# Second layer's latent attention: no norm of the latents, heads in half tiles read from PSUM, query weights in buffers of their own

## What is computed

```python
cq, ckv, kr = jnp.split(h @ w_down, [Q_LORA, Q_LORA + KV_LORA], axis=-1)
q = (rms_norm(cq, qa_g) @ w_uq).reshape(B, S, H_B, QK_NOPE + QK_ROPE)
kv = (rms_norm(ckv, kva_g) @ w_ukv).reshape(B, S, H_B, QK_NOPE + V_DIM)
k_nope, v = kv[..., :QK_NOPE], kv[..., QK_NOPE:]
k = jnp.concatenate([k_nope, jnp.broadcast_to(kr[:, :, None, :], (B, S, H_B, QK_ROPE))], axis=-1)
q = rope_tail(rms_norm(q, q_g), QK_ROPE, cos[:, None, :], sin[:, None, :])
k = rope_tail(rms_norm(k, k_g), QK_ROPE, cos[:, None, :], sin[:, None, :])
```

## Time and profile before

| | us |
|---|---|
| median of three executions | 1251.47 |
| lowest and highest | 1250.41, 1252.01 |
| the profiled execution's own time | 1252.3 |
| its span in the trace | 1250.4 |
| PE busy in the span | 1215.3 |
| VectorE (DVE) busy | 763.2 |
| ScalarE (ACT) busy | 545.9 |
| POOL busy | 216.5 |

### The profile page before, as it was taken

The page is one execution under the profiler, slowest core; times in us unless marked ns, Lnnn a source line. Parts: engine busy times, 40 slices in busy tenths (PEclk is TensorE's granted clock), DMA queues, the critical chain, the costliest instruction groups (busy, mean ns, idle before and its releaser), DMA issues.

```text
span 1250.4 us, 17161 instructions
## 1 busy us (share of the span) xinstructions
PE 1215.3 (97%) x6052; PEld 971.6 (78%) x6052; DVE 763.2 (61%) x1315; ACT 545.9 (44%) x931; POOL 216.5 (17%) x262
## 2 busy tenths in 40 slices
PE   7999999999999999999999878999999999999998
PEld 5758876678788888878888766778788888887887
DVE  4588976646766565663337778763775656664334
ACT  5554345645534343333226676643543433343222
POOL 4423433411200000000004663430400000000000
PEclk9999999999999999999999999999999999999999
DMA  6522222212322222212233100012322222212323
GB/s 234 192 93 87 83 78 60 69 51 101 108 101 94 101 101 101 84 61 91 101 101 105 50 20 1 1 35 101 130 73 101 101 101 101 90 62 84 101 92 110
DMA packets 25120, 110.83 MB, mean 89 GB/s; under 512 B 2752, under 2 KB 3136, under 8 KB 17776
## 3 DMA queue, kind: packets, MB, share of 16 engines
q1 hardware_dynamic: 25072, 110.21, 25.5%
HBM read 108.06 MB, written 6.33 MB: 91 GB/s over the span
## 4 chain that ended last, share of the span: by engine, by line
PE 88%; DVE 6%; POOL 2%; issue 2%; ACT 2%; DMA 1%; SPq 0%; DVEq 0%; POOLq 0%; ACTq 0%
PE ps L1737 25%; PE ps L1739 24%; PE ps L1738 24%; PE ps L1498 3%; PE ps L1517 3%; PE ps L1388 2%; PE ps L1376 2%; DVE h_lo L954 1%; DVE xT L1151 1%; DVE w_lo L948 1%; PE ps L1371 1%; PE ps L1482 1%; PE ps L1410 1%; PE ps L1709 1%; POOL rope_tmp L490 1%
## 5 line engine op out<-in xcount | busy, mean ns | idle before, releaser
L948 DVE TENSOR_TENSOR w_lo<-raw,w_hi 128x1024 fp32r<-128x1024 f32 (+4 forms) x114 | 195.2, 1712 | 260.9 <-ACT w_hi L582 260.9
L1737 PE MATMUL ps<-h_hi,w_hi 128*128 128x512 f32 (+1 forms) x712 | 278.6, 391 | 2.5 <-DVE w_lo L948 2.5
L582 ACT ACTIVATE w_hi<-raw 128x1024 fp32r<-128x1024 f32 (+4 forms) x124 | 177.8, 1434 | 230.3 <-PE ps L1739 230.3
L1738 PE MATMUL ps<-h_lo,w_hi 128*128 128x512 f32 (+1 forms) x712 | 277.8, 390 | 0.0
L1739 PE MATMUL ps<-h_hi,w_lo 128*128 128x512 f32 (+1 forms) x712 | 277.8, 390 | 0.0
L1737 PE MATMUL ps<-a_hi,w_hi 128*128 128x512 f32 x480 | 188.0, 392 | 2.1 <-DVE w_lo L948 1.6
L1738 PE MATMUL ps<-a_lo,w_hi 128*128 128x512 f32 x480 | 186.8, 389 | 0.0
L1739 PE MATMUL ps<-a_hi,w_lo 128*128 128x512 f32 x480 | 186.8, 389 | 0.0
L1737 PEld LDWEIGHTS ps<-h_hi,w_hi 128*128 128x128 f32 (+1 forms) x712 | 133.6, 188 | 32.1 <-DVE w_lo L948 3.4
L1738 PEld LDWEIGHTS ps<-h_lo,w_hi 128*128 128x128 f32 (+1 forms) x712 | 133.7, 188 | 28.3 <-issue 0.6
L1739 PEld LDWEIGHTS ps<-h_hi,w_lo 128*128 128x128 f32 (+1 forms) x712 | 133.5, 188 | 28.4 <-issue 0.7
(11 more groups left out here) (188 smaller groups left out, 1510.7 us busy)
## 6 DMA issues: line engine op xcount, KB each, us to landing
raw<-in_f_up SPq DMA_DIRECT2D x44, 1024.0 KB, 4.8
raw<-in_f_w_down SPq DMA_DIRECT2D x44, 512.0 KB, 3.3
raw<-in_a_in_wide SPq DMA_DIRECT2D x13, 1024.0 KB, 4.8
bias_tiles<-bias_rows SPq DMA_DIRECT2D x1, 4096.0 KB, 19.7
raw<-in_a_w_out SPq DMA_DIRECT2D x8, 512.0 KB, 3.2
raw<-in_b_w_out SPq DMA_DIRECT2D x8, 512.0 KB, 3.3
xT<-in_xt SPq DMA_DIRECT2D x4, 512.0 KB, 6.5
toep_b<-bias_tiles SPq DMA_DIRECT2D x8, 256.0 KB, 3.2
```

Of the source, the lines that this page charges most:

```text
L582: sc.activation(w_hi[:, s, 0:n], raw[:, s, 0:n], ACT.Copy).then_inc(w_hi_done, 1)
L948: dve.tensor_tensor(w_lo[:, s, 0:n], raw[:, s, 0:n], w_hi[:, s, 0:n].bitcast(F32), ALU.subtract)\
L1737: pe.matmul(dst, s_hi, m_hi, start=start, stop=False)
L1738: pe.matmul(dst, s_hi, m_lo, start=False, stop=False)
```

## The change

*Latents.* They leave PSUM without the token's root and without their norm. Their squares are taken in two instructions of two tiles each (lat_sq). The root of the latent's mean square cancels in the norm of a head except beside the 1e-6, so VectorE works out what the 1e-6 becomes and ScalarE adds it as the bias of a head's root (q_bias, k_bias). The values are scaled by the inverse root s_inv on their way out of PSUM, and the rotated key by kr_by. The gains of the latents are multiplied into the weights: three matmuls of one column in the first layer turn them into columns (g_col); ScalarE and VectorE apply them as they split the query weights, POOL to the raw key and value weights.

*Homes.* The split query weights have buffers of their own (uq_hi, uq_lo), so they are made before the down projection has ended. The key and value remainders are POOL's.

*Heads.* 16 halves w of eight heads in two banks: ScalarE copies only the query's raw tails (tails) and squares both banks; POOL rotates the tails in three steps with tables that carry the gain (rope, made in the first layer); VectorE sums, takes the reciprocal, scales the 512 plain columns from PSUM to tok96 and the 256 tails from SBUF. tok96 has two buffers. Three of four groups of turned heads are ScalarE's. The scores no longer wait group by group, since all copies are waited for ahead of them, and the sums of the token norm move to bank 7.

The diff, cut to its core:

```diff
--- before.py
+++ after.py
...
+            c_pair = sb("c_pair", [P, 3, 2, S], F32R, scope)
+            uq_hi = sb("uq_hi", [P, 2, QW], F32R, scope)
+            uq_lo = sb("uq_lo", [P, 2, QW], F32R, scope)
...
-                    chain.then_wait(pool.tensor_tensor(tail, tail, g_bq.unsqueeze(1).to_broadcast([P, H, ROT]),
-                                                       ALU.mult))
-                    rotate(H, tail[:, :, 0:HALF], tail[:, :, HALF:ROT], *tables_of(t, H), m_rot)
-                    pool.wait_ge(m_rot, g + 1)
...
+            def turned(x, j, t, done):
+
+                n = x.shape[1]
+                t1, t2 = (rope_tmp[:, a, 0:n * ROT].rearrange("p (h d) -> p h d", d=ROT) for a in range(2))
+                by_cos, by_sin = (rope[:, 2 * j + a, t, :].unsqueeze(1).to_broadcast([P, n, ROT]) for a in range(2))
+                pool.tensor_tensor(t1, x, by_cos, ALU.mult)
+                chain.then_wait(pool.tensor_tensor(
+                    t2.rearrange("p h (a f) -> p h a f", a=2), x.rearrange("p h (a f) -> p h a f", a=2)[:, :, ::-1, :],
+                    by_sin.rearrange("p h (a f) -> p h a f", a=2), ALU.mult))
+                pool.tensor_tensor(x, t1, t2, ALU.add).then_inc(done, 1)
+
+            for k in range(2):
+                pool.wait_ge(w_raw[k], 8 * (U_B + 4) + 16)
+                pool.tensor_scalar(raw[:, k, 0:D], raw[:, k, 0:D], g_col[:, 0:1], 1.0, ALU.mult, ALU.mult)\
+                    .then_inc(kv_scaled, 1)
+            for w in range(Q_HALVES):
+                pool.wait_ge(m_tail, w + 1)
+                turned(tails[:, w % 2], 0, w // 2, m_rot)
+                pool.wait_ge(m_rot, w + 1)
+                if w % 2:
+                    t = w // 2
+                    pool.wait_ge(pb_sq, t // 2 + 1)
+                    turned(lat[:, t, Q_LORA + KV_LORA:B_DOWN].unsqueeze(1), 1, t, pb_krot)
+                    pool.wait_ge(pb_krot, t + 1)
+                if w in (2, 4):
+                    pool_lo(U_B + 3 + w // 2)
...
+            chain.then_wait(sc.activation(g_col[:, 0:3], ps[:, 7, G_COL_AT:G_COL_AT + 3], ACT.Copy))
...
-                        hi(U_B + 2, (pb_half, 1))
+                        for k in range(2):
+                            sc.wait_ge(w_raw[k], 8 * (U_B + 2) + 16)
+                            sc.activation(uq_hi[:, k, :], raw[:, k, 0:QW], ACT.Identity, scale=g_col[:, 1 + k:2 + k])\
+                                .then_inc(w_hi_done, 1)
...
+            def raw_tails(w):
+
+                sc.wait_ge(m_mm, w + 1)
+                if w >= 2:
+                    sc.wait_ge(m_tok, w - 1)
+                sc.activation(tails[:, w % 2].rearrange("p (c h) d -> p c h d", c=2), both_banks(w, DH, DB), ACT.Copy)\
+                    .then_inc(m_tail, 1)
+
+            def head_squares(w):
+
+                n = DB if w < Q_HALVES else DH
+                sc.wait_ge(m_mm, w + 1)
+                if w:
+                    sc.wait_ge(m_red, w)
+                sc.activation(b_sq[:, 0:HH * n].rearrange("p (c h d) -> p c h d", c=2, d=n), both_banks(w, 0, n),
+                              ACT.Square).then_inc(m_sq, 1)
...
+            for w in range(HALVES + 2):
+                if w in (2, 4):
+                    sc.wait_ge(kv_scaled, w // 2)
+                    hi(U_B + 3 + w // 2, (pb_done, T))
+                if w == 6:
+                    sc.wait_ge(k_bias_ok, 1)
+                    sc.activation(s_kv, s_sq, ACT.Sqrt).then_inc(s_kv_ok, 1)
+                if w < Q_HALVES:
+                    raw_tails(w)
+                if w < HALVES:
+                    head_squares(w)
+                if Q_HALVES <= w < HALVES:
+                    if w == Q_HALVES:
+                        sc.wait_ge(s_inv_ok, 2)
+                    values(w)
+                if w == 0:
+                    latents_hi(3)
+                if w >= 2:
+                    turned_heads(w - 2)
+                if w < HALVES:
+                    head_roots(w)
...
+            def upper_less(k):
+
+                dve.wait_ge(w_hi_done, U_B + 3 + k)
+                dve.scalar_tensor_tensor(uq_lo[:, k, :], raw[:, k, 0:QW], g_col[:, 1 + k:2 + k],
+                                         uq_hi[:, k, :].bitcast(F32), ALU.mult, ALU.subtract).then_inc(w_lo_done, 1)
...
-                for j, cols in enumerate((slice(0, Q_LORA), slice(Q_LORA, Q_LORA + KV_LORA))):
-                    dve.scalar_tensor_tensor(lat[:, t, cols], lat[:, t, cols], small[:, t, 4 + j:5 + j],
-                                             g_lat[:, cols], ALU.mult, ALU.mult).then_inc(pb_lat, 1)
+                dve.tensor_copy(lat[:, t, :], ps[:, t, 0:B_DOWN]).then_inc(pb_raw, 1)
...
+            def k_biases():
+
+                dve.tensor_reduce(sum_kv, lat_sq[:, :, Q_LORA:Q_LORA + KV_LORA], AX, ALU.add)
+                chain.then_wait(dve.tensor_reduce(sum_kr, lat_sq[:, :, Q_LORA + KV_LORA:B_DOWN], AX, ALU.add))
+                dve.tensor_scalar(sum_kv, sum_kv, 1.0 / KV_LORA, None, ALU.mult)
+                chain.then_wait(dve.tensor_tensor(sum_kr, sum_kr, m_inv, ALU.mult))
+                dve.scalar_tensor_tensor(s_sq, m_tok2, EPS, sum_kv, ALU.mult, ALU.add)
+                chain.then_wait(dve.tensor_scalar(sum_kr, sum_kr, 1.0 / DB, EPS, ALU.mult, ALU.add))
+                dve.tensor_tensor(k_bias, sum_kr, s_sq, ALU.mult).then_inc(k_bias_ok, 1)
...
+            upper_less(0)
+            upper_less(1)
             latents_raw(0)
             latents_raw(1)
-            latents_normed(0)
+            token_rstd(2)
+            dve.tensor_tensor(m_tok2, std[:], std[:], ALU.mult)
...
-                    dve.tensor_tensor(tok[:, hh, :], tok[:, hh, :],
-                                      hf[:, g % 2, hh].unsqueeze(2).to_broadcast([P, H // parts, DB]), ALU.mult)\
-                        .then_inc(m_tok, 1)
...
+            def normed_heads(w):
+
+                g, half = w // 2, w % 2
+                n = 4 * (DB if w < Q_HALVES else 2 * DH)
+                dve.wait_ge(m_root, w + 1)
+                chain.then_wait(dve.reciprocal(hf[:, w % 2, 0:HH], hr[:, w % 2, 0:HH]))
+                if w >= 4:
+                    dve.wait_ge(m_tp, w - 3)
+                tok = tok96[:, g % 2, half * HH * DB:(half + 1) * HH * DB]
+                dve.tensor_tensor(tok.rearrange("p (c h d) -> p c h d", c=2, d=DB)[:, :, :, 0:DH],
+                                  ps[:, 2 * half:2 * half + 2, 0:n].rearrange("p c (h d) -> p c h d", h=4)[:, :, :, 0:DH],
+                                  hf[:, w % 2, 0:HH].rearrange("p (c h) -> p c h", c=2).unsqueeze(3)
+                                  .to_broadcast([P, 2, 4, DH]), ALU.mult).then_inc(m_nope, 1)
+                if w < Q_HALVES:
+                    dve.wait_ge(m_rot, w + 1)
+                    source = tails[:, w % 2]
+                else:
+                    dve.wait_ge(pb_krot, g - T + 1)
+                    source = lat[:, g - T, Q_LORA + KV_LORA:B_DOWN].unsqueeze(1).to_broadcast([P, HH, ROT])
+                by = 1.0 if w < Q_HALVES else kr_by[:, g - T:g - T + 1]
+                dve.scalar_tensor_tensor(tok.rearrange("p (h d) -> p h d", d=DB)[:, :, DH:DB], source, by,
+                                         hf[:, w % 2, 0:HH].unsqueeze(2).to_broadcast([P, HH, ROT]),
+                                         ALU.mult, ALU.mult).then_inc(m_tok, 1)
+
+            for w in range(HALVES + 2):
+                if w < HALVES:
+                    head_sums(w)
+                if w == 0:
                     latents_lo(3)
-                if g == 3:
-                    lo(U_B + 5)
-                if 1 <= g < 9 and g != 7:
-                    normed_heads(g - 1)
+                if w == 1:
+                    q_biases(1)
+                if w == 2:
+                    k_biases()
+                if w == Q_HALVES - 1:
+                    dve.wait_ge(s_kv_ok, 1)
+                    dve.reciprocal(s_inv, s_kv).then_inc(s_inv_ok, 1)
+                    dve.tensor_tensor(kr_by, s_kv, rstd[:], ALU.mult).then_inc(s_inv_ok, 1)
+                if w == Q_HALVES:
+                    dve.wait_ge(s_inv_ok, 2)
+                if w >= 2 and w % 2:
+                    turned_heads(w - 2)
+                if w < HALVES:
+                    normed_heads(w)
...
+                            for j, at in enumerate(LAT_AT):
+                                ins = pe.matmul(ps[:, 7, G_COL_AT + j:G_COL_AT + j + 1], g_lat[:, at:at + P],
+                                                ident[:, 0:1], start=True, stop=True)
...
+            def head_product(w):
+
+                g, half = w // 2, w % 2
+                tok = slice((g % T) * P, (g % T + 1) * P)
+                pe.wait_ge(pb_clo, g % T + 1)
+                if w < 2:
+                    pe.wait_ge(pb_raw, 2 * half + 2)
+                else:
+                    pe.wait_ge(m_nope, w - 1)
+                    if w - 2 < Q_HALVES:
+                        pe.wait_ge(m_tail, w - 1)
+                    else:
...
```

(68 more changed lines are left out.)

357 lines of the change are left out of this document (112 added, 245 removed).

## The result

The changed kernel takes 1268.69 us (median of 4, 1268.32 to 1269.78); the kernel before took 1251.63 beside it. The ratio is 1.0137, with a 95% interval of 1.0124 to 1.015. So it is 17.1 us slower, where 1245.6 was forecast. All of its runs lie above the range.

The account below looks back on a forecast made before the run. PE, busy 97% of the span, was taken as the bound, with the second layer's heads a latency chain whose saving reaches the end. -6.5 + 0.6 = -5.9 gave 1246.4 profiled, 1245.6 us as median; range 1240.5 to 1250.3.

Parts of the forecast that it names:

- rival 3: At the key arithmetic PE falls to its low clock and stays there: first score at 765, 1257 us; chance 0.06.
- the list of what would show the forecast wrong: Signs: even pace, norm row over 0.8 us, first query product after 699, low clock through query halves, later attention gaps.
- Front: Second layer's latents up to the first query product: a draw, 697.4 against 697.08.
- the clock's zero: Granted clock in the second layer's heads: new idle behind the third half costs the old 1.4 us, so zero change.
- Query halves: Second layer's query heads: POOL leads with 3.5 us per half, its sum 28.1, rotations from 700.1 to 730.6.
- k_biases: Small key arithmetic on VectorE at half 2: its banks come free about 4 us later, POOL idles 2.4 us.
- Norm and tails: VectorE's norm from PSUM, 0.6 to 0.9 us, and tails, 0.33 to 0.6, per half; low ends taken.
- Rival 2: VectorE's chain as slow as the old one, norm 0.9 and tails 0.6: 1252.0, no change; chance 0.13.
- rival 1: Short VectorE instructions slip between POOL's without holds: first score at 748.1, 1240.3 us; chance 0.18.
- Key halves: Loop through VectorE and ScalarE, 2.45 us per half: tok96 complete at 752.3, first score at 753.4, 6.5 us earlier.
- First layer: Three one-column matmuls fetching the gains add 0.6 us on the path; rope operations and the gains' copy cost zero.
- Rival 4: Behind the stage, attention or the output weights take the time back: 1251.5 us; chance 0.03.

Follow-up runs that it names:

- e1: Changed kernel with an unused 32-byte tile ahead of v, so later tiles lie as in the kernel before: 1245.96 us, ratio 0.9964.
- g1: e1 with the two weight remainders computed by VectorE instead of POOL, behind the norms of halves 3 and 5: 1243.28 us, ratio 0.9934.

## Why the prediction was wrong

**The step that failed** is in the first paragraph: "Here its work stays the same, so I look for waits." PE's products in the rest of the program did stay the same; their price, which the sum put at nothing without a reason, didn't. The 4,200 matmuls that stream 512 columns in the blocks became 6 ns longer, 24.9 us of busy time, through 32 bytes in the placement of the tiles; giving these back took 22.7 us off the kernel (e1). No rival held it: rival 3, the slower one, looked for the loss in the changed stage, and so did the list of what would show the forecast wrong. With the distance given back the changed kernel takes 1245.96 us beside 1250.8, where the sum had said 5.9 us less: 4.8.

The other steps, by e1's trace, in which they stand alone:

- *Front.* First query product forecast at 697.4, found at 698.91. There the granted clock was 0.62 from 692 to 696 (1.00 in the kernel before), so partly at the lower level of 1.2 GHz, behind a wait of PE of 2.81 us; in g1, where it was 1.00, the product stands at 697.51. The step was right, the clock's zero cost 1.4 us.
- *Query halves.* POOL's first rotation 2.9 us behind the first product (forecast 2.7), the last one complete at 732.36, 30.6 us behind the start of the first (forecast 30.5). The sum is right by luck: POOL idled 1 us more than forecast and worked 0.9 less (next item).
- *k_biases.* Forecast 4 us with both TENSOR_SCALARs free; 4.4 us from 709.62 to the reciprocal at 713.99. The sum nearly came out, its terms did not: the first of the two was held for the whole remainder (2.19), and the two-tensor ones behind it then found it gone (0.15) or met a rotation (0.58, 0.57). The rule of the Trainium skill that stood against the row at 733.92 (GPSIMD Engine Reference, "Specifications": also a two-port mode contends) stands, and this trace agrees with it: 2.19 beside POOL's remainder, 0.17 without. The row at 733.92 was misread: it ends at 734.16, and POOL's instruction of 733.39 at 734.12, so it had waited too, only briefly. POOL idled 3.4 us behind half 2 instead of 2.4, and its own sum came out shorter by as much.
- *Norm and tails.* Rows of 0.69 and 0.41, 0.61 and some 0.35 from start to start, near the low ends that were taken (0.6 and 0.33). Rival 2 (0.9 and 0.6) is out. So is rival 1, no holds: the tails beside the second remainder took 2.17, at 722.15.
- *Key halves.* 2.50 us each (norms from 734.66 to 752.19, seven steps), forecast 2.45. tok96 complete at 753.3 (forecast 752.3), first score at 754.46 (753.4), 5.4 us earlier than before, not 6.5: the front's 1.5, of which the rest won back 0.4.
- *First layer.* Forecast +0.6; the down products begin at 672.42, 0.1 us earlier than before. The added matmuls take 0.8 at 21.93 and PE is 0.44 late behind them, but a wait at 32 takes it back: by 35 it is level with the kernel before. Zero would have been right.
- *Rival 4*, that the gain doesn't reach the end: from the first score to the end 490.6 us in both. Out. *Rival 3*, a low clock through the query halves: it fell behind the third half, as feared, but for one half only (3.5 us instead of 2.2). Out.
